# A 64-wide recurrence scan: the selection of F's halves on GpSimd instead of VectorE, with a new order of all pieces

## What is computed

```python
def step(S, inp):
    r_t, w_t, k_t, v_t, a_t, b_t = inp
    sa = jnp.einsum("bhvk,bhk->bhv", S, a_t)
    S = S * w_t[:, :, None, :] + sa[..., :, None] * b_t[..., None, :] + v_t[..., :, None] * k_t[..., None, :]
    return S, jnp.einsum("bhvk,bhk->bhv", S, r_t)
o_f, s_f = _wkv7_scan(r_h, decay_h[0], k_dir[0], v_h, -kk, kk * iclr_h[0], s0_f, False)
o_b, s_b = _wkv7_scan(r_h, decay_h[1], k_dir[1], v_h, -kk, kk * iclr_h[1], s0_b, True)
```

## Time and profile before

| | us |
|---|---|
| three timed runs, median (lowest to highest) | 3328.45 (3325.11 to 3330.67) |
| the profiled execution | 3316.46 |
| its span, first to last instruction | 3314.8 |
| PE / VectorE / ScalarE / GpSimd busy in the span | 2814.3 / 1460.3 / 687.0 / 239.9 |
| mean granted TensorE clock | 0.92 |

### The profile page before, as it was taken

How to read it: one execution, slowest core, us unless ns; L and a number is a source line. 1 busy time by engine, 2 the same in 40 slices (tenths; PEclk the granted TensorE clock), 3 DMA queues, 4 the chain that set the end, 5 groups by cost and what they waited for, 6 DMA issues and landing times. The chain is left out here.

```text
span 3314.8 us, 74741 instructions
## 1 busy us (share of the span) xinstructions
PE 2814.3 (85%) x33346; PEld 1716.8 (52%) x33346; DVE 1460.3 (44%) x2235; ACT 687.0 (21%) x1247; POOL 239.9 (7%) x379
## 2 busy tenths in 40 slices
PE   7499999996887887793999999957889888888697
PEld 1155555552343443441555555536777777777543
DVE  0222222224666667104100000039898989898301
ACT  0122212210000000002000000134545454544100
POOL 0000000000000000000000000001112111112100
PEclk9699999998888988896999999968999999999798
DMA  6232222223210210411223222210111111110141
GB/s 252 103 90 85 87 89 85 82 72 112 61 60 32 69 55 0 174 57 45 87 75 110 93 94 92 93 44 27 33 40 37 44 33 44 34 43 23 38 166 60
DMA packets 207155, 241.88 MB, mean 73 GB/s; under 512 B 21991, under 2 KB 157687, under 8 KB 204584
## 3 DMA queue, kind: packets, MB, share of 16 engines
q1 hardware_dynamic: 196332, 195.90, 18.9%
q0 software_dynamic: 10560, 41.95, 3.4%
HBM read 184.32 MB, written 53.49 MB: 72 GB/s over the span
## 5 line engine op out<-in xcount | busy, mean ns | idle before, releaser
L104 PE MATMUL ps<-mix,rw 128*128 128x512 f32 (+1 forms) x2048 | 562.7, 438 | 23.2 <-DMA rw<-in_rw_w_k 7.0
L104 PE MATMUL ps<-hT,hw 128*128 128x512 f32 (+1 forms) x2048 | 561.2, 435 | 6.2 <-DMA hw<-in_hy_w_in 6.2
L104 PEld LDWEIGHTS ps<-mix,rw 128*128 128x128 f32 x2048 | 313.1, 193 | 272.8 <-issue 272.8
L104 PEld LDWEIGHTS ps<-hT,hw 128*128 128x128 f32 x2048 | 312.5, 191 | 252.2 <-issue 252.2
L104 PE MATMUL ps<-ow,oy 128*128 128x512 f32 x640 | 281.1, 602 | 28.4 <-DMA oy<-scratch_y_d 21.6
L1325 POOL TENSOR_SCALAR e_Sd<-e_S,e_pcd 128x64 f32<-128x64 f32 x256 | 163.0, 653 | 777.4 <-DVE e_S L107 310.9
L104 PEld LDWEIGHTS ps<-ow,oy 128*128 128x128 f32 x640 | 123.1, 193 | 185.4 <-issue 162.2
L118 ACT ACT_TABLE_LOAD x90 | 115.5, 1283 | 378.5 <-PE ps L104 275.8
L107 DVE SCALAR_TENSOR_TENSOR mix<-xx,col,hT 128x640 f32<-128x640 f32 x48 | 38.6, 879 | 287.9 <-PE ps L104 287.9
L104 PE MATMUL ps<-hsd,dft 128*128 128x512 f32 x288 | 139.3, 647 | 29.4 <-DVE hsd L115 29.4
L112 DVE TENSOR_SCALAR hcv<-hpad,hpc 128x641 f32<-128x641 f32 x48 | 29.5, 616 | 305.5 <-ACT hpad L118 305.5
(11 more groups left out here) (206 smaller groups left out, 4179.6 us busy)
## 6 DMA issues: line engine op xcount, KB each, us to landing
hw<-in_hy_w_in SPq DMA_DIRECT2D x64, 512.0 KB, 4.1
aw<-in_ada_w SPq DMA_DIRECT2D x16, 1536.0 KB, 7.3
scratch_rkvz_d<-rout POOLq DMA_DIRECT2D x64, 320.0 KB, 3.4
scratch_vx_d<-hot POOLq DMA_DIRECT2D x32, 320.0 KB, 3.1
ow<-in_hy_w_out SPq DMA_DIRECT2D x32, 256.0 KB, 2.8
rw<-in_rw_w_r SPq DMA_DIRECT2D x16, 512.0 KB, 3.9
rw<-in_rw_w_k SPq DMA_DIRECT2D x16, 512.0 KB, 4.0
rw<-in_rw_w_v SPq DMA_DIRECT2D x16, 512.0 KB, 4.0
```

What stands on the lines that cost most here:

```text
L104: return nc.tensor.matmul(out, lhsT, rhs, start=first, stop=last)
```

## The change

The piece M1 moves from VectorE's block to GpSimd's: the same multiplication (five times a pair, 128 x 640), now as gpsimd.tensor_tensor, waiting for VectorE's F as before; Y on TensorE waits for GpSimd's count instead of VectorE's. GpSimd walks M1 and Sd in the list's order. ORDER, with the same 158 pieces, is replaced as a whole; in the diff, "..." stands for the old list, which is in the code above. Among other places: Q opens the slot (late 2 instead of 1 at the end), sb 1 and sb 2 and sums of the next pair close it, scan(1) stands between F0 and T(1), scan(0) behind Z*(1), out behind Z*(2), ar(0) between Y*(3) and Z*(3), kd(0) behind S*(6), and at the fifth level bonus_in, tilde(1) and ar(1) stand between Z*(4) and bonus*, with Y before T on TensorE where it was behind it.

```diff
--- before.py
+++ after.py
@@ -1129,24 +1129,24 @@
     has_next = lambda s, m: not (s == "s" and m == CS - 1)
     step_of = {(d, c): (n, s, m, q) for n, chains in enumerate(STEPS) for s, d, m, c, q in chains}
 
...
+    ORDER = [("W*", 1, 0), ("Q", 2), ("sums*", 1), ("U", 1, 0), ("U*", 1, 0), ("lora", 1, 0, 0), ("sb*", 1, 1), ("sb*", 1, 2), ("S", 1, 0),
+             ("sb", 1, 0), ("std", 1), ("lora*", 1, 0, 0), ("S*", 1, 0), ("W", 1, 1), ("W*", 1, 1), ("sb*", 1, 0), ("C", 1), ("rstd", 1),
+             ("tb", 1, 1), ("F0", 1), ("lora", 1, 0, 1), ("U", 1, 1), ("Sd", 1, 1), ("U*", 1, 1), ("S", 1, 1), ("lora*", 1, 0, 1), ("S*", 1, 1),
+             ("M1", 1, 1), ("CT", 1), ("tb*", 1, 1), ("CT*", 1), ("scan", 1, 1), ("T", 1, 1), ("W", 1, 2), ("T*", 1, 1), ("W*", 1, 2), ("sk", 1, 0),
+             ("lora", 1, 1, 0), ("sk*", 1, 0), ("U", 1, 2), ("U*", 1, 2), ("sk", 1, 1), ("sk*", 1, 1), ("wider", 1, 0), ("S", 1, 2),
+             ("lora*", 1, 1, 0), ("tb", 1, 0), ("Sd", 1, 2), ("spread", 1, 0), ("tb*", 1, 0), ("Y", 1, 1), ("S*", 1, 2), ("Y*", 1, 1), ("W", 1, 3),
+             ("W*", 1, 3), ("sk", 1, 2), ("U", 1, 3), ("spread*", 1, 0), ("Z", 1, 1), ("Sd", 1, 3), ("lora", 1, 1, 1), ("U*", 1, 3), ("sk*", 1, 2),
+             ("S", 1, 3), ("Z*", 1, 1), ("V", 1), ("lora*", 1, 1, 1), ("S*", 1, 3), ("wider", 1, 1), ("W", 1, 4), ("scan", 1, 0), ("M1", 1, 2),
+             ("T", 1, 2), ("spread", 1, 1), ("W*", 1, 4), ("T*", 1, 2), ("V*", 1), ("spread*", 1, 1), ("U", 1, 4), ("Y", 1, 2), ("Sd", 1, 4),
+             ("U*", 1, 4), ("Y*", 1, 2), ("S", 1, 4), ("Z", 1, 2), ("exps", 1, 1), ("b0", 1, 1), ("tk", 1, 0), ("S*", 1, 4), ("b0", 1, 0),
+             ("Z*", 1, 2), ("W", 1, 5), ("Sd", 1, 5), ("out", 1), ("W*", 1, 5), ("tk*", 1, 0), ("U", 1, 5), ("T", 1, 3), ("T*", 1, 3), ("M1", 1, 3),
+             ("U*", 1, 5), ("S", 1, 5), ("S*", 1, 5), ("Y", 1, 3), ("exps", 1, 0), ("ka", 1, 0), ("W", 1, 6), ("W*", 1, 6), ("Y*", 1, 3),
+             ("Z", 1, 3), ("ar", 1, 0), ("Sd", 1, 6), ("Z*", 1, 3), ("U", 1, 6), ("tk", 1, 1), ("ka", 1, 1), ("U*", 1, 6), ("S", 1, 6), ("S*", 1, 6),
+             ("tk*", 1, 1), ("M1", 1, 4), ("T", 1, 4), ("kd", 1, 0), ("fin", 1), ("W", 1, 7), ("Y", 1, 4), ("T*", 1, 4), ("Y*", 1, 4), ("W*", 1, 7),
+             ("tilde", 1, 0), ("U", 1, 7), ("kd", 1, 1), ("U*", 1, 7), ("Z", 1, 4), ("O", 1), ("Z*", 1, 4), ("bonus_in", 1), ("tilde", 1, 1),
+             ("M1", 1, 5), ("fin*", 1), ("bonus", 1), ("ar", 1, 1), ("bonus*", 1), ("O*", 1), ("Y", 1, 5), ("W", 0, 0), ("T", 1, 5), ("keys", 0),
+             ("Sd", 0, 0), ("Y*", 1, 5), ("T*", 1, 5), ("center", 0), ("Z", 1, 5), ("sb", 0, 1), ("center*", 0), ("sums", 0), ("Z*", 1, 5),
+             ("sb", 0, 2)]
     OF = {}
     for base, names in ((MAIN, "sb sb* sk sk* V V* tb tb* tk tk* C F0 CT CT* T T* Y Y* Z Z* M1 Q"), (CHAIN, "W W* U U* S S* Sd O O* fin fin*"),
                         (POST, "center center* out"), (PREP, "keys lora lora* scan exps b0 ka kd tilde ar bonus_in bonus bonus*"),
@@ -1323,7 +1323,12 @@
                             wait(dv_, "end", i, 1)
                         u = unit(d, c)
                         po_.did(nc.gpsimd.tensor_scalar(Sd[:, q, :], S_at[:, n, q, :], pcd[i % 3][:, u:u + 1], None, MUL), ("Sd", i, n))
-                walk({"Sd": decayed})
+
+                def choose(i, lv):
+
+                    wait(dv_, "F", i, lv)
+                    po_.did(nc.gpsimd.tensor_tensor(M1[:, :, :], F, spread_over(chosen[:, lv, :], NC), MUL), ("M1", i, lv))
+                walk({"Sd": decayed, "M1": choose})
 
             @block.tensor
             def _(pe):
@@ -1394,7 +1399,7 @@
 
                 def across(i, lv):
                     wait(ac_, "took", "CT", i)
-                    wait(dv_, "M1", i, lv)
+                    wait(po_, "M1", i, lv)
                     pe_.did(product(pair_free("Y", i, lv), lambda p: CT[:, p, :], lambda p: M1[:, p, :]), ("Y", i, lv))
 
                 def joined(i, lv):
@@ -1680,10 +1685,6 @@
                     wait(dv_, "F-", i)
                     dv_.did(tt(F, F, spread_over(eye2, NC), ADD), ("F", i, 1))
 
-                def choose(i, lv):
-                    wait(dv_, "F", i, lv)
-                    dv_.did(tt(M1[:, :, :], F, spread_over(chosen[:, lv, :], NC), MUL), ("M1", i, lv))
-
                 def turn_f(i, lv):
                     wait(pe_, "T", i, lv)
                     src = pair_of(("T", i, lv), 5 * C).rearrange("p g (c n) -> p g c n", n=C)
@@ -1820,7 +1821,7 @@
                     dv_.did(tt(bon[j % 3][:, :], wide[:, 0:T], v[:, :], MUL), ("took", "bonus", j))
                     dv_.note(("bonus", j))
                 dv_.did(ts(omka[:, :], col[:, 3, K_A * KE:(K_A + 1) * KE], -1.0, 1.0, MUL, ADD), ("omka",))
-                walk({"sb*": scores("sb"), "sk*": scores("sk"), "C": both_ways, "F0": first_level, "M1": choose, "T*": turn_f, "Y*": across,
+                walk({"sb*": scores("sb"), "sk*": scores("sk"), "C": both_ways, "F0": first_level, "T*": turn_f, "Y*": across,
                       "Z*": joined, "Q": triangles, "S*": next_state, "scan": scan, "sums*": sums, "rstd": rstd, "spread*": spread,
                       "out": out, "b0": key_rate, "kd": key_dir, "tilde": tilde, "ar": ar, "bonus_in": bonus_in, "bonus*": bonus_out})
```

More of the change, by code:

```diff
@@ L1130, in rwkv_scan @@
     step_of = {(d, c): (n, s, m, q) for n, chains in enumerate(STEPS) for s, d, m, c, q in chains}
-    ORDER = [("center*", 1), ("sums", 1), ("sb", 1, 0), ("sums*", 1), ("lora", 1, 0, 0), ("W*", 1, 0), ("sb*", 1, 1), ("U", 1, 0), ("std", 1),
[14 rows of a table removed]
-             ("bonus_in", 1), ("tilde", 1, 1), ("tilde", 1, 0), ("ar", 1, 1), ("M1", 1, 5), ("fin*", 1), ("bonus", 1), ("Sd", 0, 0), ("T", 1, 5),
-             ("O*", 1), ("W", 0, 0), ("bonus*", 1), ("T*", 1, 5), ("Y", 1, 5), ("Y*", 1, 5), ("center", 0), ("Z", 1, 5), ("Z*", 1, 5), ("Q", 1),
-             ("keys", 0), ("sb", 0, 1)]
+    ORDER = [("W*", 1, 0), ("Q", 2), ("sums*", 1), ("U", 1, 0), ("U*", 1, 0), ("lora", 1, 0, 0), ("sb*", 1, 1), ("sb*", 1, 2), ("S", 1, 0),
[17 rows of a table added]
     OF = {}
```

## The result

The change makes the kernel slightly slower: 3335.16 us against 3324.2, medians of 20 runs each, ratio 1.0036 [1.0023, 1.0049], some 12 us. The forecast was 3357, +29. The direction and the kind of mechanism held, the size did not. TensorE's granted clock in the scan's steady stretch is 0.98 after and was 0.96 before; what goes with that is told under "Where TensorE counts".

The account below looks back on a forecast made before the run. VectorE was taken to pace some 41 us of a 54.8 us slot, a VectorE-PE chain the other 14. +1.7 a slot made +23, with end slots +29: 3345.5 in the profile, 3357 us as median; range 3286 to 3395.

Parts of the forecast that it names:

- four M1 off VectorE: Dense part of a slot: four M1 instructions leave VectorE, each worth 0.735 us, -2.94 us a slot.
- four blocks: Behind M1(1) to M1(4), VectorE's two-input instructions stand while GpSimd reads: +2.9 us a slot.
- fifth level: From M1(5)'s old starting point to Z*, GpSimd and TensorE's chain take 5.7 us instead of 4.89: +0.8 a slot.
- waits before S*(3), S*(6): New order leaves VectorE too little work between states, so it waits: at most 1.8 us a slot, taken as +0.9.
- C: The forecast: VectorE's two-input instructions stand while GpSimd reads, at four places a slot; 3338 to 3395 us, chance 0.55.
- A: Rival: no exclusion of weight, M1 and VectorE run side by side; 51.0 us a slot, 3281 us, chance 0.28.
- B: Rival: only GpSimd waits, VectorE never does; blocks 0, 3329 us, no change, chance 0.17.
- M1 waits until bonus: Fifth level: GpSimd's M1(5) gets in only after bonus_in, tilde(1) and ar(1), when VectorE reads PSUM.
- The head: Q, sums*, the sb* and S*(0) stand against the same TensorE work: 0, allowing -0.5 to +0.5 us.
- First and last slot: Each M1 takes longer where VectorE is less full: +4 us in the last slot, +2 in the first pair's.
- The rate of exchange: VectorE sets the pace for some 41 us of a slot, counted one for one; a mixed chain the other 14.
- The order by itself: New order of pieces, apart from M1's engine: 13 us for its waits and nothing for its head.

Follow-up runs that it names:

- e3: Changed kernel with two fills on GpSimd, about as long and reading nothing, in place of each M1: 3328.35 us, 1.0002 of the kernel before.
- e8: Kernel before (old order) with all five M1 on GpSimd, Sd(6) moved ahead of M1(4) and b0(1) behind T*(4): 3321.02 us, 0.9991.
- e7: Kernel before (old order) with M1 of levels 1 to 4 on GpSimd, Sd(6) ahead of M1(4), b0(1) behind T*(4): 3322.1 us, 0.9998.
- e15: Changed kernel with level 5's M1 back on VectorE: 3339.87 us, 1.0047 of the kernel before.
- e5: Kernel before (old order) without M1, its tile filled once ahead of the scan: 3310.59 us, 0.9964.
- e1: Kernel before with the new order alone, M1 still on VectorE: 3349.71 us, 1.0062.
- e6: New order without M1, its tile filled once ahead of the scan: 3321.52 us, 0.9991 of the kernel before.
- e9: Kernel before with 80 of O's products left out on TensorE (1.17 us a slot): 3297.73 us, 0.9927.
- e10: Kernel before without M1 and with 80 of O's products left out (e9 together with e5): 3275.04 us, 0.9847.
- e16: Changed kernel with kd(0) moved behind Y*(4), and Y(4) ahead of W(7) and fin on TensorE: 3330.78 us, 1.0025 of the kernel before.
- e17: Same two moves as e16, with M1 not computed at all: 3315.56 us, 0.9976 of the kernel before.
- e2: Kernel before (old order) with all five M1 on GpSimd, nothing else changed: 3321.82 us, 0.9986.
- e11: Kernel before with 0.95 us a slot of TensorE's tk transposes left out mid-slot: 3318.28 us, 0.9986.
- e4: Kernel before (old order) with M1 of levels 1 to 3 on GpSimd, the others on VectorE: 3317.92 us, 0.9971.

## Why the prediction was off

The kind was right, the size not. By the forecast's own steps, a slot (means over 14 slots of the two profiles):

| | forecast | measured in the trace after |
|---|---|---|
| four M1 off VectorE | -2.94 | -2.94 |
| four blocks | +2.9 | +2.4 (the two scans 1.34 together, out 0.87, kd 0.19) |
| fifth level | +0.8 | 0.0 |
| waits before S*(3), S*(6) | +0.9 | +0.7 |
| sum | +1.7 | +0.2 |
| the slot itself | +1.7 | +0.4 |

- **Exclusion (C against A and B)**: right in kind and place. VectorE's instructions with two SBUF inputs stand while GpSimd reads; e3 shows that it is the reads. Three of the four blocks came as forecast; kd's is 0.19 for 0.55, since S*(6) waits first and kd is issued only some 0.4 us before M1(4) ends (2704.62 and 2704.99 in one slot).
- **The fifth level is the step that failed**, 0.8 of the 1.5 by which the sum was too high. "M1 waits until bonus*" was carried over from an Sd that had stood for three multiplies. M1 gets in after one (0.5 us later than asked) and holds up tilde for 1.12. From the end of ar to Z* it is now 3.9, and 5.0 with the block, against 5.0 before (4.89 in the one slot that the forecast read). Two pairs of runs price it at nothing as well: e8 against e7 (0.9991 and 0.9998, where +0.8 a slot would be 11 us) and the changed kernel against e15 (1.0036 and 1.0047). Even the delay there is bounded by TensorE, which is at O until M1(5) is long done; the earlier trace rows showed the packed stretch, but the forecast began to count it only when M1 was ready.
- **S* waits**: 0.7 for 0.9, nearly all of it before S*(6) (0.59; 0.09 before S*(3), where the forecast had more than half). Another 0.58 came before Y*(1), which it had not.
- **The head** was set at 0 within 0.5. S*(0) comes 1.1 earlier after Z*(5), but F0 is complete 10.3 us after Q against 10.4, so next to nothing comes of it for the levels.
- **First and last slot**: +6 forecast, +0.4 measured. In the profile's terms 17 of the missing 23 us (+29 forecast, +6.2 measured) lie in the 14 slots and 6 here.
- **The rate of exchange** is the error behind the sum, and only the runs show it. The forecast read the slot as 41 us of VectorE, counted one for one, and 14 of a mixed chain. M1's 59 us on VectorE are worth 12 in the old order (e5) and 24 in the new one (e1 to e6), and the 49 us of blocks are worth 11 (e3). O and what follows on TensorE share the end (e9, e10).
- **The order by itself** had 13 us for its waits and nothing for its head; the 0.8 of the fifth level was order and GpSimd together. e1 has it at 21, and about half of that goes with Y(4)'s place on TensorE (e16, e17), which was never priced, since the forecast compared only VectorE's list of the fourth level. Where it had four M1 against four blocks at zero, the changed kernel is 9 us faster than e1. That the total came out on the forecast side is so in part luck: the order cost more than it was given, and GpSimd less.
- **TensorE's clock** had no term. It is 0.96 before and 0.98 after in the steady stretch, and 0.921 over the whole program after, against 0.916 to 0.918 of the kernel before in the later sessions. By the 2.0 us for 0.001 of above, an estimate, 6 to 10 of the 17 us by which the median fell short came from there; at full clock the slots differ by 1.1 us (53.1 and 54.2) and not by 0.4. The forecast's +1.7 is above that too.

VectorE's whole slot does close: five M1 off (-3.7), five blocks (+3.5), and idle time up from 5.3 to 5.9 (767 less 693.4, and less 684.5, over 14) make +0.4. That is no proof that each term counts in full. The terms are stretches of VectorE's line, and the waits among them take up what is gained or lost elsewhere.

## What to carry to other kernels

Before a microsecond of a busy engine is priced at a microsecond, ask which engine is packed from there to the end of the loop: leave out the operation altogether in one run and see what is the most that moving it can give (here 12 us of 59 in the old order, 24 in the new). Do that in the order that will be used. In this kernel a two-input operation on GpSimd took its reading time from VectorE's two-input instructions (1.12 us from tilde); it was cheap only where VectorE next read PSUM (e2's scans kept 1481 ns), and it must not stand in GpSimd's queue ahead of something small that a chain waits for (2.5 us a slot in e2). A new order should be compared on every engine's list: here the piece that hurt was behind two others on TensorE, while VectorE's list looked fuller. And differences of a few microseconds should be read beside the granted clock of the runs compared (e11).

## What was not expected of the hardware

- A small and a large GpSimd instruction fare differently against back-to-back VectorE instructions with two SBUF inputs: an Sd stood for 2.0 us through three of them, M1(5) only until the running one had ended (2711.99, 1.84 us in all, 0.5 of it waiting). Why is open; the two differ in having one input stream or two.
- An M1 with two streams of 640 takes 1.32 us on GpSimd, a fill of as many 0.632.
- TensorE's pauses for issue come to 15 to 62 us in 767 (14.6 in e9, 24.1 in e2, 30.5 before, 35.4 after, 48.9 in e4, 56.1 in e3, 61.8 in e17). They grow when M1 is taken out of a kernel, but do not follow VectorE's load alone; their cause is not settled.
- The granted clock was higher in the slower kernel: TensorE was busy 669 of 767 us at a clock of 0.96 before, and 651 at 0.98 after.
